# Attention heads issued in pairs on TensorE: scores in one step, values in the next

## The chip, the cores and the metric

The kernel runs on one core of one Trainium2 chip. The metric is the device time of one execution in microseconds. The kernel before took 1118.67 us in the median of three runs (1115.35, 1126.55 and 1118.67); the profiled execution, from which every row below comes, took 1115.28 us, of which 1113.6 us are its span.

## The reference

A trunk of two layers on 256 tokens of width 1024, all in fp32. Each layer is: half a SwiGLU, a mixer, half a SwiGLU, and a gated embedding; at the end a norm. The change concerns the mixers. Each has 16 heads of width 64:

```
# even layer (layer 0)
oa = forgetting_attention(...)        # 8 heads: softmax(q k / 8 + F_q - F_k, causal) v
ob = stick_breaking_attention(...)    # 8 heads: exp(log_sigmoid(z) + reversed running sum) v, no softmax
# odd layer (layer 1)
oc = chunked_relbias_attention(...)   # 8 heads: softmax(q k / 8 + bias[rel]) v
od = sliding_window_gqa(...)          # 8 query heads on 2 key/value heads, ALiBi, a sink in the softmax
x = x + concatenate([o_first, o_second]) @ w_out
```

For every head the kernel needs scores (q times k, contraction over the head's 64 dimensions, 128 + 256 columns for two row blocks of 128 tokens), something that makes weights of them, and values (weights times v: contraction over 128 tokens, 64 output dimensions, 256 + 128 columns).

## The kernel before

**Precision and storage.** The large products are split: weights and activations are each kept as a high and a low fp32r part, and a product is three matmuls (lines 1063 to 1065, helper `product`, and 1168 to 1170 in `token_tile`). The attention's own matmuls are plain fp32. In the trace each fp32 matmul stands as two MATMUL records, each behind a LDWEIGHTS record of its own; a transpose stands as one. q and k lie transposed (`qT`, `kT`: 128 partitions are the dimensions of two heads), so head 2p has partitions 0 to 63 and head 2p + 1 partitions 64 to 127 of the same tile. The output of values is transposed as well: head 2p writes partitions 0 to 63 and head 2p + 1 partitions 64 to 127 of one PSUM bank, and the even or odd pair picks the bank (`BANK_O`).

**Order of the work.** Each engine has its own program, written out by hand, and semaphores tie them. On TensorE the input projection (`mixer_in`) makes tiles of 128 output columns, each 24 matmuls; between the tiles lie attention steps. `attention_step(layer, i)` runs for i = 0 to 18. In layer 0 steps 0 to 11 each follow a tile of the input projection (the last 12 of 24 tiles), in layer 1 steps 0 to 10 (the last 11 of 19). The rest lie in `mixer_out`: there each step holds a half tile of the output projection (12 matmuls, `out_half`), passed in as `tile`, which is issued after the step's scores and ahead of the rest. Step i issues, in this order: the scores of head i, the tile if there is one, the middle part of head i - 1, the values of head i - 2.

**The middle part** is, for softmax heads, three transposes of the normalised weights (line 1263) into one bank, which ScalarE copies to `probsT` (line 670); for stick-breaking heads (layer 0, heads 8 to 15) it is three fp32 matmuls onto the scores' bank (1269 to 1271), whose exponential ScalarE writes to `probsT` (line 676). Scores of stick-breaking heads begin with two bf16 matmuls that write the mask (1248, 1249).

**The other engines.** VectorE (attention_step from line 930) evicts the tile, adds the bias and takes the row minimum of head i (line 951), splits weight chunks (746), normalises head i (965 to 970), and at even steps writes the low part of the output of a finished pair (979, semaphore `os_lo`). ScalarE takes the exponentials of head i (651, or 661 and 663), then copies head i - 1 to `probsT`, then at even steps writes the high part of the pair (680), then splits weights (511). Two waits matter below. The copy to `probsT` for head j waits until the values of head j - 2, which read the same buffer, are done (`pv_done`). The scores of head j wait until the bank of head j - 2 is free: for stick-breaking that is the exponential of line 676 (`sb_a`), for softmax the bias step of line 951 (`logits_ready`).

`out_half` for the first half uses the outputs of the pairs 0 to 3; for its first tile each product waits for `os_lo` of its pair.

Of the kernel before, what the change touches and what calls it, by code (L numbers as in the profile page):

```python
# [13 lines left out]
P = 128  # L14
D_MODEL, SEQ, D_FF, D_PLE, DEPTH = 1024, 256, 2816, 256, 2
HD = 64
# [13 lines left out]
LOGITS = 3 * P  # L30
# [92 lines left out]
def trunk(nc, x, p, ln_ffn1, w_ffn1_gu, w_ffn1_down, ln_mix, w_in_even, b_forget, w_out_even, w_in_odd,  # L123
# [14 lines left out]
    with ExitStack() as ctx:  # L138
# [15 lines left out]
        with ExitStack() as region:  # L154
            osp = region.enter_context(nc.sbuf_tensor("osp", [P, KD, 2, SEQ], F32R))
            qT = region.enter_context(nc.sbuf_tensor("qT", [P, 8, SEQ], F32))
            kT = region.enter_context(nc.sbuf_tensor("kT", [P, 8, SEQ], F32))
            vN = region.enter_context(nc.sbuf_tensor("vN", [P, TOK, 2 * GROUP_W], F32))
# [21 lines left out]
        probsT = sb("probsT", [P, 2, LOGITS], F32)  # L180
# [5 lines left out]
        mask_sb = sb("mask_sb", [P, P], BF16)  # L186
        identb = sb("identb", [P, P], BF16)
# [31 lines left out]
        ps = ctx.enter_context(nc.psum_tensor("ps", [P, 8, 512], F32))  # L219
        BANK_S, BANK_PT, BANK_F = 4, 6, 7  # L220
        BANK_O = (3, 7)
# [25 lines left out]
        scores_done, logits_ready = sem("scores_done"), sem("logits_ready")  # L247
        exp_done, pt_done, pt_ready = sem("exp_done"), sem("pt_done"), sem("pt_ready")
        sb_abs, sb_e, sb_log, sb_sp, incl_done, sb_a = sem("sb_abs"), sem("sb_e"), sem("sb_log"), sem("sb_sp"), sem("incl_done"), sem("sb_a")
        norm_step, probs_ready, pv_done = sem("norm_step"), sem("probs_ready"), sem("pv_done")  # L250
# [23 lines left out]
        heads = [(layer, group, h) for layer in range(DEPTH) for group in range(2) for h in range(HEADS)]  # L274
        is_sb = [layer == 0 and group == 1 for layer, group, h in heads]
        soft_no = [sum(not s for s in is_sb[:g]) for g in range(len(heads))]
        stick_no = [sum(is_sb[:g]) for g in range(len(heads))]

        def head_q(g):
            _, group, h = heads[g]  # L280
            r = HD * (h % 2)
            return slice(r, r + HD), 4 * group + h // 2

        def head_k(g):
            layer, group, h = heads[g]
            if layer == 1 and group == 1:
                return 4 if h // 4 == h % 2 else 5
            return 4 * group + h // 2

        def head_v(g):  # L290
            layer, group, h = heads[g]
            return GROUP_W * group + HD * (h // 4 if layer == 1 and group == 1 else h)
# [41 lines left out]
        def last_written(layer, want):  # L334

            return written(layer, max(n for n, t in enumerate(IN_TILES[layer]) if want(t[2], t[3])))
# [712 lines left out]
        def _(pe):  # L1049
# [178 lines left out]
            def scores(g):  # L1228
                layer, group, h = heads[g]
                s, (rows, qt), kt = g % 2, head_q(g), head_k(g)  # L1230
                S = ps[:, BANK_S + s]

                held = 4 if layer == 1 and group == 1 else kt
                pe.wait_ge(*last_written(layer, lambda what, idx: (what, idx) in (("q", qt), ("k", held))))
                if layer == 1 and group == 1 and kt == 5:
                    pe.wait_ge(k_swapped, 32)
                if g >= 2:

                    if is_sb[g - 2]:
                        pe.wait_ge(sb_a, stick_no[g - 2] + 1)  # L1240
                    else:
                        pe.wait_ge(logits_ready, 2 * (soft_no[g - 2] + 1))
                if not is_sb[g]:
                    for t, sl, keys in ((0, slice(0, P), P), (1, slice(P, LOGITS), SEQ)):
                        mm = pe.matmul(S[:, sl], qT[rows, qt, t * P:(t + 1) * P], kT[rows, kt, 0:keys], start=True, stop=True)  # L1245
                else:

                    pe.matmul(S[:, 0:P], identb[:], mask_sb[:], start=True, stop=True)
                    pe.matmul(S[:, 2 * P:LOGITS], identb[:], mask_sb[:], start=False, stop=True, skip_group_check=True)
                    pe.matmul(S[:, 0:SEQ], kT[rows, kt, 0:P], qT[rows, qt, :], start=False, stop=True, skip_group_check=True)  # L1250
                    mm = pe.matmul(S[:, 2 * P:LOGITS], kT[rows, kt, P:SEQ], qT[rows, qt, P:SEQ], start=False, stop=True,
                                   skip_group_check=True)
                mm.then_inc(scores_done, 1)

            def middle(g):
                s = g % 2
# [14 lines left out]
                    pe.matmul(S[:, SEQ:LOGITS], negtri[:], sp_[:, SEQ:LOGITS], start=False, stop=True,  # L1271
                              skip_group_check=True).then_inc(incl_done, 1)

            def values(g):
                s, v = g % 2, head_v(g)
                layer, group, h = heads[g]
                if layer == 1 and group == 1:
                    pe.wait_ge(*last_written(layer, lambda what, idx: what == "vd"))
                else:
                    pe.wait_ge(*last_written(layer, lambda what, idx: what == "v" and idx[:2] == (group, h // 4)))  # L1280
                if is_sb[g]:
                    pe.wait_ge(sb_a, stick_no[g] + 1)
                else:
                    pe.wait_ge(pt_ready, soft_no[g] + 1)


                pair, rows = g // 2, slice(HD * (g % 2), HD * (g % 2 + 1))
                if pair % KD < 2:
                    reuse(BANK_O[pair % 2])
                else:  # L1290
                    pe.wait_ge(os_lo, pair - 1)
                V = vN[:, :, v:v + HD]
                O = ps[rows, BANK_O[pair % 2], :]
                pe.matmul(O[:, 0:SEQ], V[:, 0], probsT[:, s, 0:SEQ], start=True, stop=False)  # L1294
                pe.matmul(O[:, P:SEQ], V[:, 1], probsT[:, s, SEQ:LOGITS], start=False, stop=True).then_inc(pv_done, 1)  # L1295

            def attention_step(layer, i, norm, tile=None):

                first, n = 2 * HEADS * layer, 2 * HEADS
                g = first + i  # L1300
                if i == 0:

                    pe.wait_ge(rstd_ready, norm + 1)
                    if layer == 0:
                        pe.wait_ge(bias_ready, HEADS)
                        pe.wait_ge(f_step, 4)
                    else:
                        pe.wait_ge(p_lo, 1)
                if i < n:
                    scores(g)  # L1310
                if tile is not None:
                    tile()
                if 1 <= i <= n:
                    middle(g - 1)
                if 2 <= i <= n + 1:
                    values(g - 2)
                if i == n + 2:
                    for b in range(2):
                        reader[BANK_O[b]] = (os_lo, (first + n) // 2 - 1 + b)
# [55 lines left out]
            for m in range(KD):  # L1375
                if m >= 4:
                    pe.wait_ge(resid, m - 3)
                for t in range(TOK):
                    mm = pe.transpose(ps[:, m % 4, t * P:(t + 1) * P], xin[:, t, m * P:(m + 1) * P], ident[:])
# [55 lines left out]
```

## Time and profile before

| | |
|---|---|
| runs, us | 1115.35, 1118.67, 1126.55; median 1118.67 |
| profiled execution, us | 1115.28, span 1113.6, mean granted TensorE clock 0.989 |
| TensorE matmul (PE) | busy 1080.0 us, 97% of the span |
| TensorE weight load (PEld) | busy 953.0 us, 86% |
| VectorE (DVE) | busy 773.6 us, 69% |
| ScalarE (ACT) | busy 590.3 us, 53% |
| GpSimd (POOL) | busy 82.8 us, 7% |

Times are microseconds unless marked ns, counted from the start of the span. A line number is a line of the kernel. The ends of matmuls are modelled, so two that follow each other overlap in the rows; what a matmul takes of the engine is the distance from its start to the start of the next. A row of the timeline may hold several records of one form: its start is that of the first, its length reaches to the end of the last.

### The profile page before, as it was taken

The numbers are of one execution on the slowest core, as the hardware profiler recorded it, in microseconds if no ns is written. First come the engines' busy times: TensorE is split into PE (matmuls) and PEld (weight loads), VectorE is DVE, ScalarE is ACT, GpSimd is POOL, SyncE is SP. The second block draws the span as 40 slices with busy tenths as digits, with TensorE's granted clock in tenths as the row PEclk, the third lists the DMA queues.
The fourth block names the chain that finished last, engine by engine and source line by source line (L and its number), as shares of the span: only waits on it lengthen the run. The fifth ranks groups of instructions, "written<-read, shape, count | busy, mean of one in ns | idle before, by whom it ended". The sixth has DMA issues, their size and how long they took to land.

```text
span 1113.6 us, 18550 instructions
## 1 busy us (share of the span) xinstructions
PE 1080.0 (97%) x6691; PEld 953.0 (86%) x6691; DVE 773.6 (69%) x1361; ACT 590.3 (53%) x1027; POOL 82.8 (7%) x112
## 2 busy tenths in 40 slices
PE   4999999999999999999999999998999999999996
PEld 3888888998888888888888888888987888888886
DVE  5887855666545887855689777667657698785566
ACT  5565545434445565545556565444555566554454
POOL 4000001000002000001020000014003200000102
PEclk9999999999999999999999999999999999999998
DMA  8656447563232756447546554566623275544731
GB/s 258 217 191 204 130 139 222 186 194 114 87 104 60 234 188 208 130 137 224 189 152 227 190 187 143 154 203 207 202 81 114 85 227 187 190 129 136 212 128 39
DMA packets 225848, 183.94 MB, mean 165 GB/s; under 512 B 4648, under 2 KB 224512, under 8 KB 225792
## 3 DMA queue, kind: packets, MB, share of 16 engines
q1 hardware_dynamic: 222688, 181.45, 52.0%
q10 hardware_dynamic: 3104, 1.77, 0.6%
q8 instruction: 32, 0.52, 0.2%
q14 instruction: 24, 0.20, 0.1%
HBM read 182.02 MB, written 1.06 MB: 164 GB/s over the span
## 4 chain that ended last, share of the span: by engine, by line
PE 89%; DVE 5%; issue 3%; ACT 2%; DMA 0%; SPq 0%; DVEq 0%; POOLq 0%; POOL 0%; ACTq 0%
PE ps L1072 43%; PE ps L1073 22%; PE ps L1063 5%; PE ps L1064 4%; PE ps L1065 4%; DVE wsp L746 2%; PE ps L1245 2%; PE ps L1294 2%; PE ps L1168 1%; PE ps L1169 1%; PE ps L1170 1%; ACT wsp L511 1%; PE ps L1263 1%; PE ps L1295 1%; DMA gin<-in_ln_final_dram 0%
## 5 line engine op out<-in xcount | busy, mean ns | idle before, releaser
L746 DVE TENSOR_TENSOR wsp<-raw,wsp 128x1024 fp32r<-128x1024 f32 (+1 forms) x382 | 423.3, 1124 | 69.1 <-ACT wsp L511 62.7
L1072 PE MATMUL ps<-xsA,wsp 128*128 128x512 f32 x1056 | 372.7, 397 | 4.5 <-DVE wsp L746 3.9
L511 ACT ACTIVATE wsp<-raw 128x1024 fp32r<-128x1024 f32 (+1 forms) x382 | 356.0, 958 | 32.4 <-PE ps L1065 30.1
L1073 PE MATMUL ps<-xsA,wsp 128*128 128x256 f32 x1056 | 296.8, 281 | 0.0
L1072 PE MATMUL ps<-hff,wsp 128*128 128x512 f32 x704 | 245.4, 394 | 0.0
L1072 PEld LDWEIGHTS ps<-xsA,wsp 128*128 128x128 f32 x1056 | 198.9, 188 | 52.2 <-issue 5.2
L1073 PEld LDWEIGHTS ps<-xsA,wsp 128*128 128x128 f32 x1056 | 200.7, 190 | 0.0
L1073 PE MATMUL ps<-hff,wsp 128*128 128x256 f32 x704 | 196.7, 279 | 0.0
L1072 PEld LDWEIGHTS ps<-hff,wsp 128*128 128x128 f32 x704 | 131.9, 187 | 30.4
L1073 PEld LDWEIGHTS ps<-hff,wsp 128*128 128x128 f32 x704 | 132.8, 189 | 0.0
L1072 PE MATMUL ps<-xsB,wsp 128*128 128x512 f32 x352 | 124.2, 398 | 2.3 <-DVE xsB L810 2.1
L761 DVE TENSOR_TENSOR sq<-ps,sq 128x512 f32<-128x512 f32 x88 | 60.5, 687 | 86.0 <-ACT sq L527 86.0
L1063 PE MATMUL ps<-xsA,wsp 128*128 128x256 f32 x360 | 106.8, 297 | 3.4 <-DVE wsp L746 3.4
L571 ACT ACTIVATE xsA<-xT,gains 128x256 fp32r<-128x256 f32 x56 | 28.4, 507 | 152.1 <-DVE xT L872 126.8
L527 ACT ACTIVATE sq<-ps 128x512 f32<-128x512 f32 x88 | 51.9, 589 | 106.4 <-PE ps L1073 106.4
L1064 PE MATMUL ps<-xsA,wsp 128*128 128x256 f32 x360 | 104.0, 289 | 0.0
L1065 PE MATMUL ps<-xsA,wsp 128*128 128x256 f32 x360 | 103.8, 288 | 0.0
L1073 PE MATMUL ps<-xsB,wsp 128*128 128x256 f32 x352 | 98.1, 279 | 0.0
L1072 PEld LDWEIGHTS ps<-xsB,wsp 128*128 128x128 f32 x352 | 66.7, 190 | 18.5 <-DVE xsB L810 2.6
L530 ACT ACTIVATE silu<-gate_n 128x256 f32<-128x256 f32 x88 | 36.8, 419 | 84.9 <-DVE gate_n L763 84.9
L1063 PEld LDWEIGHTS ps<-xsA,wsp 128*128 128x128 f32 x360 | 71.2, 198 | 5.8 <-DVE wsp L746 3.6
L1064 PEld LDWEIGHTS ps<-xsA,wsp 128*128 128x128 f32 x360 | 71.3, 198 | 0.1
(172 smaller groups left out, 1328.4 us busy)
## 6 DMA issues: line engine op xcount, KB each, us to landing
raw<-in_w_ffn_gu_dram SPq DMA_DIRECT2D x88, 1024.0 KB, 5.1
raw<-in_w_ffn_down_dram SPq DMA_DIRECT2D x64, 704.0 KB, 4.7
raw<-in_w_in_even_dram SPq DMA_DIRECT2D x12, 1024.0 KB, 5.4
raw<-in_w_in_odd_dram SPq DMA_DIRECT2D x9, 1024.0 KB, 5.3
raw<-in_w_ple_gate_dram SPq DMA_DIRECT2D x8, 1024.0 KB, 5.9
raw<-in_w_out_even_dram SPq DMA_DIRECT2D x4, 1024.0 KB, 5.2
raw<-in_w_out_odd_dram SPq DMA_DIRECT2D x4, 1024.0 KB, 5.2
raw<-in_w_ple_proj_dram SPq DMA_DIRECT2D x2, 1024.0 KB, 5.1
```

What stands on the lines that cost most here:

```text
L511: act.activation(wsp[:, s, 0, half * n:(half + 1) * n], raw[:, s, half * n:(half + 1) * n], ACT.Copy).then_inc(hi, 1)
L527: act.activation(cross[:], ps[:, b:b + 3:2, SEQ:], ACT.Copy).then_inc(gu_cross, 1)
L530: act.activation(silu[:], gate_n[:, 0], ACT.Silu).then_inc(gu_silu, 1)
L571: act.activation(stream(norm)[:, m, 0, :], xT[:, m], ACT.Copy, scale=gain(norm, m)).then_inc(xs_hi, 1)
L746: dve.tensor_tensor(wsp[:, s, 1, sl], raw[:, s, sl], wsp[:, s, 0, sl].bitcast(F32), ALU.subtract).then_inc(lo, 1)
L761: dve.tensor_tensor(cross[:], ps[:, b:b + 3:2, 0:SEQ], cross[:], ALU.add).then_inc(gu_sum, 1)
L1063: pe.matmul(out_, whi, moving[:, 0, :], start=first, stop=False)
L1064: pe.matmul(out_, whi, moving[:, 1, :], start=False, stop=False)
L1065: return pe.matmul(out_, wlo, moving[:, 0, :], start=False, stop=last)
L1072: pe.matmul(ps[:, bank, :], whi, moving.rearrange("p s t -> p (s t)"), start=first, stop=False)
L1073: return pe.matmul(ps[:, bank, SEQ:], wlo, moving[:, 0, :], start=False, stop=last)
L1245: mm = pe.matmul(S[:, sl], qT[rows, qt, t * P:(t + 1) * P], kT[rows, kt, 0:keys], start=True, stop=True)
```

## The change

Softmax heads' scores are issued for two heads at once, at even steps (`scores_pair`): first the 128-column part of head g, then that of head g + 1, then the 256-column parts in the same order. The scores of stick-breaking heads stay one head a step (`scores`). Values of all heads are issued for two heads at once, at odd steps from step 3 on (`values_pair`, for heads i - 3 and i - 2): the 256-column parts of both, then the 128-column parts of both. The waits follow: a pair of scores waits for `logits_ready` of head g - 1, and a pair of values for the `probsT` of both heads. The middle part, the programs of the other engines and the number of matmuls are as before.

```diff
--- before.py
+++ after.py
@@ -1230,27 +1230,37 @@
                 s, (rows, qt), kt = g % 2, head_q(g), head_k(g)
                 S = ps[:, BANK_S + s]
 
-                held = 4 if layer == 1 and group == 1 else kt
-                pe.wait_ge(*last_written(layer, lambda what, idx: (what, idx) in (("q", qt), ("k", held))))
-                if layer == 1 and group == 1 and kt == 5:
+                pe.wait_ge(*last_written(layer, lambda what, idx: (what, idx) in (("q", qt), ("k", kt))))
+                if is_sb[g - 2]:
+                    pe.wait_ge(sb_a, stick_no[g - 2] + 1)
+                else:
+                    pe.wait_ge(logits_ready, 2 * (soft_no[g - 2] + 1))
+
+                pe.matmul(S[:, 0:P], identb[:], mask_sb[:], start=True, stop=True)
+                pe.matmul(S[:, 2 * P:LOGITS], identb[:], mask_sb[:], start=False, stop=True, skip_group_check=True)
+                pe.matmul(S[:, 0:SEQ], kT[rows, kt, 0:P], qT[rows, qt, :], start=False, stop=True, skip_group_check=True)
+                pe.matmul(S[:, 2 * P:LOGITS], kT[rows, kt, P:SEQ], qT[rows, qt, P:SEQ], start=False, stop=True,
+                          skip_group_check=True).then_inc(scores_done, 1)
+
+            def scores_pair(g):
+
+                layer, group, h = heads[g]
+                kinds = [("q", head_q(g)[1])] + [("k", 4 if layer == 1 and group == 1 else head_k(g))]
+                pe.wait_ge(*last_written(layer, lambda what, idx: (what, idx) in kinds))
+                if layer == 1 and group == 1:
                     pe.wait_ge(k_swapped, 32)
                 if g >= 2:
-
-                    if is_sb[g - 2]:
-                        pe.wait_ge(sb_a, stick_no[g - 2] + 1)
+                    if is_sb[g - 1]:
+                        pe.wait_ge(sb_a, stick_no[g - 1] + 1)
                     else:
-                        pe.wait_ge(logits_ready, 2 * (soft_no[g - 2] + 1))
-                if not is_sb[g]:
-                    for t, sl, keys in ((0, slice(0, P), P), (1, slice(P, LOGITS), SEQ)):
-                        mm = pe.matmul(S[:, sl], qT[rows, qt, t * P:(t + 1) * P], kT[rows, kt, 0:keys], start=True, stop=True)
-                else:
-
-                    pe.matmul(S[:, 0:P], identb[:], mask_sb[:], start=True, stop=True)
-                    pe.matmul(S[:, 2 * P:LOGITS], identb[:], mask_sb[:], start=False, stop=True, skip_group_check=True)
-                    pe.matmul(S[:, 0:SEQ], kT[rows, kt, 0:P], qT[rows, qt, :], start=False, stop=True, skip_group_check=True)
-                    mm = pe.matmul(S[:, 2 * P:LOGITS], kT[rows, kt, P:SEQ], qT[rows, qt, P:SEQ], start=False, stop=True,
-                                   skip_group_check=True)
-                mm.then_inc(scores_done, 1)
+                        pe.wait_ge(logits_ready, 2 * (soft_no[g - 1] + 1))
+                for t, sl, keys in ((0, slice(0, P), P), (1, slice(P, LOGITS), SEQ)):
+                    for e in (g, g + 1):
+                        rows, qt = head_q(e)
+                        mm = pe.matmul(ps[:, BANK_S + e % 2, sl], qT[rows, qt, t * P:(t + 1) * P], kT[rows, head_k(e), 0:keys],
+                                       start=True, stop=True)
+                        if t == 1:
+                            mm.then_inc(scores_done, 1)
 
             def middle(g):
                 s = g % 2
@@ -1271,28 +1281,30 @@
                     pe.matmul(S[:, SEQ:LOGITS], negtri[:], sp_[:, SEQ:LOGITS], start=False, stop=True,
                               skip_group_check=True).then_inc(incl_done, 1)
 
-            def values(g):
-                s, v = g % 2, head_v(g)
+            def values_pair(g):
+
                 layer, group, h = heads[g]
                 if layer == 1 and group == 1:
                     pe.wait_ge(*last_written(layer, lambda what, idx: what == "vd"))
                 else:
                     pe.wait_ge(*last_written(layer, lambda what, idx: what == "v" and idx[:2] == (group, h // 4)))
                 if is_sb[g]:
-                    pe.wait_ge(sb_a, stick_no[g] + 1)
+                    pe.wait_ge(sb_a, stick_no[g] + 2)
                 else:
-                    pe.wait_ge(pt_ready, soft_no[g] + 1)
-
-
-                pair, rows = g // 2, slice(HD * (g % 2), HD * (g % 2 + 1))
+                    pe.wait_ge(pt_ready, soft_no[g] + 2)
+                pair = g // 2
                 if pair % KD < 2:
                     reuse(BANK_O[pair % 2])
                 else:
                     pe.wait_ge(os_lo, pair - 1)
-                V = vN[:, :, v:v + HD]
-                O = ps[rows, BANK_O[pair % 2], :]
-                pe.matmul(O[:, 0:SEQ], V[:, 0], probsT[:, s, 0:SEQ], start=True, stop=False)
-                pe.matmul(O[:, P:SEQ], V[:, 1], probsT[:, s, SEQ:LOGITS], start=False, stop=True).then_inc(pv_done, 1)
+                for e in (g, g + 1):
+                    rows = slice(HD * (e % 2), HD * (e % 2 + 1))
+                    pe.matmul(ps[rows, BANK_O[pair % 2], 0:SEQ], vN[:, 0, head_v(e):head_v(e) + HD], probsT[:, e % 2, 0:SEQ],
+                              start=True, stop=False)
+                for e in (g, g + 1):
+                    rows = slice(HD * (e % 2), HD * (e % 2 + 1))
+                    pe.matmul(ps[rows, BANK_O[pair % 2], P:SEQ], vN[:, 1, head_v(e):head_v(e) + HD], probsT[:, e % 2, SEQ:LOGITS],
+                              start=False, stop=True).then_inc(pv_done, 1)
 
             def attention_step(layer, i, norm, tile=None):
 
@@ -1306,14 +1318,16 @@
                         pe.wait_ge(f_step, 4)
                     else:
                         pe.wait_ge(p_lo, 1)
-                if i < n:
+                if i < n and is_sb[g]:
                     scores(g)
+                elif i < n and i % 2 == 0:
+                    scores_pair(g)
                 if tile is not None:
                     tile()
                 if 1 <= i <= n:
                     middle(g - 1)
-                if 2 <= i <= n + 1:
-                    values(g - 2)
+                if i >= 3 and i % 2 == 1:
+                    values_pair(g - 3)
                 if i == n + 2:
                     for b in range(2):
                         reader[BANK_O[b]] = (os_lo, (first + n) // 2 - 1 + b)
```

## Rows read from the trace of the kernel before

**Rows 1.** The page: busy time of engines, then chain of waits.

```profile
PE 1080.0 (97%) x6691; PEld 953.0 (86%) x6691; DVE 773.6 (69%) x1361; ACT 590.3 (53%) x1027; POOL 82.8 (7%) x112
...
PE 89%; DVE 5%; issue 3%; ACT 2%; DMA 0%; SPq 0%; DVEq 0%; POOLq 0%; POOL 0%; ACTq 0%
```

**Rows 2.** PE's waits by releaser, 300:345 (total, times, longest).

```profile
PE ps L1248 <- ACT probsT L676: 0.4, 1, 0.4
```

**Rows 3.** Windows, PE alone, layer 0's steps 0, 1, 3 (length, busy).

```profile
256.52:260.41 3.89, 3.89 (x28) 1.00 0.03 10
260.41:264.61 4.20, 4.20 (x32) 1.00 0.06 10
...
269.81:275.00 5.19, 5.19 (x37) 1.00 0.22 60
```

**Rows 4.** Timeline, PE, scores of layer 0's step 0 (start, length, operation).

```profile
256.10 0.28 PE L1064 MATMUL ps<-xsA,wsp 128*128 128x256 f32 x1
256.22 0.28 PE L1065 MATMUL ps<-xsA,wsp 128*128 128x256 f32 x1
256.52 0.89 PE L1245 MATMUL ps<-kT,qT 64*128 64x128 f32 x4
257.34 0.39 PE L1063 MATMUL ps<-xsA,wsp 128*128 128x256 f32 x1
257.57 0.28 PE L1064 MATMUL ps<-xsA,wsp 128*128 128x256 f32 x1
```

**Rows 5.** Timeline of PE, layer 1's step 10, one head's scores, transposes, values.

```profile
842.04 0.92 PE L1245 MATMUL ps<-kT,qT 64*128 64x128 f32 x4
842.89 0.55 PE L1263 MATMUL ps<-ident,probs 128*128 128x128 f32 x3
843.37 0.65 PE L1294 MATMUL ps<-probsT,vN 128*64 128x256 f32 x2
843.85 0.38 PE L1295 MATMUL ps<-probsT,vN 128*64 128x128 f32 x2
844.16 0.92 PE L1245 MATMUL ps<-kT,qT 64*128 64x128 f32 x4
```

**Rows 6.** Weight loads (PEld) of the same scores and values.

```profile
842.04 0.52 PEld L1245 LDWEIGHTS ps<-kT,qT 64*128 64x128 f32 x4
...
843.64 0.35 PEld L1295 LDWEIGHTS ps<-probsT,vN 128*64 128x64 f32 x2
```

**Rows 7.** Lines by form, scores and values (count; busy, mean ns).

```profile
L1245 PE MATMUL ps<-kT,qT 64*128 64x256 f32 x48 | 14.3, 377 | 0.0
...
L1295 PE MATMUL ps<-probsT,vN 128*64 128x128 f32 x64 | 12.2, 273 | 0.0
```

**Rows 8.** Timeline of PE, layer 0, end of step 12 and start of 13.

```profile
319.77 0.65 PE L1294 MATMUL ps<-probsT,vN 128*64 128x256 f32 x2
...
320.56 0.23 PE L1248 MATMUL ps<-mask_sb,identb 128*128 128x128 bf16 x1
```

**Rows 9.** Timeline of ACT, exponentials after the middle of steps 12, 13.

```profile
319.88 0.49 ACT L676 ACTIVATE probsT<-ps 128x384 f32<-128x384 f32 x1 [0.82 <-PE ps L1271]
...
324.33 0.47 ACT L676 ACTIVATE probsT<-ps 128x384 f32<-128x384 f32 x1
```

**Rows 10.** Timeline of PE, layer 1, the waiting product of step 11.

```profile
846.52 0.39 PE L1063 MATMUL ps<-osp,wsp 128*128 128x256 f32 x1 [0.18 <-DVE osp L979]
```

**Rows 11.** Timeline of DVE, layer 1, steps 9 to 12.

```profile
836.95 0.42 DVE L903 SCALAR_TENSOR_TENSOR qT<-ps,rstd 128x256 f32<-128x256 f32 x1 [0.87 <-PE ps L1065]
...
840.32 0.63 DVE L970 TENSOR_SCALAR probs<-probs,rinv 128x128 f32<-128x128 f32 x2
...
846.06 0.41 DVE L979 TENSOR_TENSOR osp<-ps,osp 128x256 fp32r<-128x256 f32 x1
...
850.90 0.34 DVE L951 CUSTOM_DVE_ANT_0 probs<-ps,bias_swa,nsink 128x128 f32<-128x128 f32 x1
...
853.09 0.55 DVE L970 TENSOR_SCALAR probs<-probs,rinv 128x128 f32<-128x128 f32 x2
```

## The prediction

> **What bounds the kernel now.** I read the page first: TensorE is busy 97% of the span, and the chain of waits lies on it for 89% [rows 1]. The next question is whether it is also the bound inside the mixers, where the change lies. TensorE's waits there are few: one of 0.4 us in layer 0 (the scores of head 12 wait for line 676) [rows 2], and one of 0.18 us idle, with a restart behind it, in layer 1 (step 11's product waits for line 979) [rows 10]. The windows of single steps show TensorE busy for all of 3.89, 4.20 and 5.19 us [rows 3]. So a microsecond taken from TensorE's queue in the mixers shortens the span until another engine's result is late.
>
> Where the time of a step goes is read from starts. In the projection a record of 256 columns follows the last after 0.12 us. Into the scores it is 0.30 us, the scores take 0.82 us to the next group, and the record after that comes 0.23 us later instead of 0.12 [rows 4]. Inside the scores the loads of four records span 0.52 us, the last one being 0.19 long, so they follow each other at 0.11 us [rows 6]. That is also what a 128-column fp32 record takes. The last 256-column record starts 0.92 - 0.38 = 0.54 us in and the next group at 0.85, so 0.31 lies between them [rows 5, 7]; 0.54 is an exposed first load (0.10), two steps of 0.11 and one of 0.22. **Bare streaming of one head's scores** is thus 2 x 0.11 + 2 x 0.215 = 0.65 us. The rest appears wherever the shape used of the array changes (128 x 128, 64 x 128 for scores, 128 x 64 for values): about 0.09 us after the last record, and a weight load that nothing hides, 0.10 us for 128 columns and 0.05 for 64 (the two 256-column records of values take 0.48 us, not 0.43 [rows 5]). Step 0 is one tile (24 x 0.12 = 2.87) and one visit to the scores, 3.89 - 2.87 = 1.02, so the two shape changes of that visit cost 0.36. Step 1 adds transposes, 0.31, about bare streaming: they share the tile's shape. Step 3 adds values, 5.19 - 4.20 = 0.99, of which 0.34 are shape changes [rows 3].
>
> **The change, part by part.**
>
> Fewer shape changes. Twelve visits for scores (24 softmax heads in pairs) and sixteen for values (32 heads) go away: 12 x 0.36 + 16 x 0.34 = 9.8 us. In layer 1's part of the output projection values are followed directly by scores and share a change; there are 5 such seams before and 2 after, so 3 x 0.17 = 0.5 is not gained. **9.3 us.** No wait and no instruction is added for it; the streaming of the second head stays, 0.65 us.
>
> Work on two halves. No row shows matmuls on different halves of the array next to each other, so this is bounded from both sides. Upper end of gain: starts stay in order, weight loads stay 0.11 (128 columns) or 0.05 us apart, each half does one record at a time, but the second record of one matmul and the first of the next run side by side. For scores the starts are then 0, 0.21, 0.32, 0.43, 0.54, 0.76, 0.77, 0.98 and the next group at 1.29 instead of 1.50: 0.21 a pair, little because the loads are the bound. For values 0, 0.27, 0.28, 0.49, 0.50, 0.61, 0.71, 0.82, next group at 1.02 instead of 1.44: 0.43 a pair. In all 12 x 0.21 + 16 x 0.43 = 9.4 us. Lower end: each of the three changes of half in a pair costs what a change of shape does, 0.19 (scores) and 0.14 (values): 12 x 3 x 0.19 + 16 x 3 x 0.14 = 13.6 us of loss. In between: nothing, if records only queue. I take the **gain of 9.4 us**, because the nearest rows show loading ahead at work whenever the shape stays: loads 0.19 us long follow each other at 0.11 under the matmuls [rows 6], and loads and matmuls are busy for 86% and 97% of one span [rows 1].
>
> The same rows set a rule against half of this. The Trainium skill, in "TensorE: Matmul & The Clock Gate", Part 3, says that a weight load overlaps a running matmul only when the row group differs; the halves for values share the row group. By that the values' 6.9 us would be nothing and the sum 8 us. The trace disagrees with it where the whole array is used: there too loads and matmuls run at once [rows 1].
>
> New waits in layer 0's output part (steps 11 to 16). The scores of head g wait for the exponential of head g - 2, which ScalarE starts after the middle part of the step before. Before, 0.79 us of values lay between that middle part and the scores [rows 8], and the exponential (0.49 us, beginning 0.11 us after the values did [rows 8, 9]) was ready at 320.37 with the mask at 320.56: just covered. After, even steps hold no values, so at the start of steps 13 and 15 TensorE stands still for about 0.75 us. At the end of odd steps the exponential also waits until head g - 4's values are read, which now are the first of the pair in the same step: finished 1.3 us after the pair begins without overlap (0.9 with it), exponential and signals 0.6, pair over at 1.44 (1.02): 0.5 us at the starts of steps 12 and 14, where 0.4 stood at the first. Together 2.5 less the old 0.4: **2.1 us lost.** Inside the input projection a tile of 2.87 us lies between, and nothing waits.
>
> Layer 1, step 11. The fourth product waits for `os_lo` of the fourth pair, which VectorE writes at 846.06 + 0.41 after the whole chain of step 10 [rows 11]; TensorE came at 846.2 and went on at 846.52 [rows 10]. That chain starts from head 10's scores, now 0.22 us later (two records of head 11 lie ahead of its second part). TensorE now does only the pair of scores (1.50), transposes (0.39) and nine products (1.08) from 842.04 on and arrives at 845.0; it goes on at 846.75. **1.3 us lost** against the free-running sum, 1.5 with overlap. After it VectorE paces: head 12's normalised weights come at 853.09 + 0.55 = 853.64 from a bias step at 850.90 that follows VectorE's own queue, not TensorE [rows 11]. TensorE reaches them at 853.9 without overlap, at 853.3 with it: 0.3 lost with overlap.
>
> What costs nothing, and its cover. In layer 1's projection steps the chain of head 8 and later is longest: eviction at 836.95 to 840.95, 4.0 us [rows 11], 4.2 with the later scores; TensorE needs scores, transposes and the next tile first, 1.3 to 1.5 + 0.33 + 2.87 = 4.5 to 4.7. Cover 0.3 us; gone, every such step would wait. ScalarE's copy to `probsT` at odd steps now waits for the first head of the pair in the same step, about 1.8 us after the tile, but its own exponentials end about there, 2.0 us after; the weight splits queued behind it do not move. DMAs are untouched.
>
> Sum, likeliest case: 9.3 + 9.4 - 2.1 - 1.8 = **14.8 us** less than 1115.28, that is 1100.5. The profiled execution equals the lowest run and lies 3.4 us below the median; I put half of it on top: **1102**.
>
> **The rivals** (times with the same 2 us on top).
>
> *No overlap.* Records on different halves queue at 0.11 and 0.215 us. 9.3 - 2.1 - 1.3 = 5.9: 1111. For: every pair of neighbours in the trace queues. Against: none of them is on different halves. Chance 0.24.
>
> *Scores overlap, values don't* (the rule above): 9.3 + 2.5 - 2.1 - 1.6 = 8.1: 1109. Chance 0.10.
>
> *Changing halves drains* (the other sign). Place: the three changes in each of 28 pairs, 84 in all. Price 0.14 to 0.19 us each: -5.9 + 13.6 = +7.7: 1125. It decides from 5.9 / 84 = 0.07 us per change. For: a change of shape does cost that. Against: here only the place changes. Chance 0.12. The Trainium skill, "TensorEngine Tiling (Array Packing)", Key Properties, says that changing the mode drains and changing the tile does not; its first half agrees with [rows 4, 5], no row here shows the second.
>
> *Waits eat the overlap.* The 0.3 us of cover in layer 1's projection steps is too small and VectorE paces, there and in layer 0's output part: 5 us more in waits, 1107. For: both are near in [rows 11]. Against: softmax heads without a sink have a shorter chain. Chance 0.08.
>
> **How the numbers follow.** The forecast has 0.46. A measurement of this kernel can tell about 1% (11 us) from no change. The overlap case lies 15 us off, so most of it is faster: 0.42, and 0.03 from the others; slower by over 1% needs the drain at its upper price or something I have not seen: 0.08; the rest, 0.47, is within 1%. The range takes in overlap, none, and the waits, with the median's scatter of a few us, and leaves out the drain: 1098 to 1122.
>
> **What would show it.** After: in a pair, the first 256-column record of head g + 1 starts about 0.01 us after the second of head g (overlap) or 0.215 (none) or more than 0.3 (drain). Two steps of layer 0 take 10.39 us now and should take 9.06 (9.70, 10.6). TensorE's waits should show the mask matmul of stick-breaking scores waiting for line 676 four times, 2.5 us, and step 11's product about 1.5 to 1.7 us. Wrong would be the prediction if stages outside the mixers change by more than 2 us, or if line 951 or 970 releases TensorE.

## The result, and the profile after

The changed kernel took 1101.44 us in the median of four runs (1099.68 to 1107.96), the kernel before 1119.14 us of four (1115.35 to 1126.55): a ratio of 0.985, interval 0.981 to 0.988. Timed again later beside the kernel before on another chip the ratio was 0.983 (0.979 to 0.987). The profiled execution took 1100.13 us, span 1097.3.

The waits of TensorE in the whole span, of the changed kernel (total, times, longest), those that lie in the mixers:

```profile
PE ps L1239 <- ACT probsT L676: 2.8, 4, 0.7
...
PE ps L1273 <- DVE probs L970: 2.3, 3, 1.2
...
PE ps L1063 <- DVE osp L979: 2.0, 1, 2.0
```

Before there stood 0.4 us in the first of these three lines [rows 2], nothing in the second, and 0.18 us in the third [rows 10]. The waits outside the mixers are the same in both kernels within 0.1 us, but for the first of all, for a DMA, 9.8 us here and 9.1 before. Now one pair, the timeline of PE in layer 0's step 2 and the following step 3, and PEld for the same stretches:

```profile
266.04 0.28 PE L1065 MATMUL ps<-xsA,wsp 128*128 128x256 f32 x1
266.25 0.93 PE L1260 MATMUL ps<-kT,qT 64*128 64x128 f32 x8
...
270.36 0.49 PE L1273 MATMUL ps<-ident,probs 128*128 128x128 f32 x3
270.78 0.65 PE L1302 MATMUL ps<-probsT,vN 128*64 128x256 f32 x4
271.26 0.39 PE L1306 MATMUL ps<-probsT,vN 128*64 128x128 f32 x4
271.58 0.39 PE L1063 MATMUL ps<-xsA,wsp 128*128 128x256 f32 x1
```

```profile
266.25 0.52 PEld L1260 LDWEIGHTS ps<-kT,qT 64*128 64x128 f32 x8
...
270.78 0.20 PEld L1302 LDWEIGHTS ps<-probsT,vN 128*64 128x64 f32 x4 [0.17 <-issue]
271.05 0.36 PEld L1306 LDWEIGHTS ps<-probsT,vN 128*64 128x64 f32 x4
```

Eight records of scores take 0.93 us where four took 0.92, and from the first values to the second (256 columns, then 128) it is 0.48 us for two heads as for one [rows 5]. The loads show the same: eight in 0.52 us, as four did [rows 6]. The second head of a pair costs TensorE almost nothing. From the first start to the next group a pair of scores takes 0.856 us (one head: 0.850) and a pair of values 0.800 (one head: 0.794). Two steps of layer 0, as windows of PE (stretch, length, busy time and records, granted clock, DMA share, GB/s):

```profile
266.25:270.40 4.15, 4.15 (x37) 1.00 0.83 255
270.40:274.65 4.25, 4.25 (x38) 1.00 0.17 47
```

Together 8.40 us, against 2 x 5.19 [rows 3].

**The mixers, measured alone.** From the first scores of a layer to the first matmul behind its last values, the kernel before ends at these rows of PE, layer 0 (from 256.52, [rows 4]) and layer 1:

```profile
339.35 0.39 PE L1063 MATMUL ps<-osp,wsp 128*128 128x256 f32 x1
...
792.89 0.37 PE L1245 MATMUL ps<-kT,qT 64*128 64x128 f32 x1
...
867.75 0.39 PE L1063 MATMUL ps<-osp,wsp 128*128 128x256 f32 x1
```

and the changed kernel at

```profile
259.12 0.38 PE L1260 MATMUL ps<-kT,qT 64*128 64x128 f32 x2
...
333.07 0.39 PE L1063 MATMUL ps<-osp,wsp 128*128 128x256 f32 x1
...
786.88 0.38 PE L1260 MATMUL ps<-kT,qT 64*128 64x128 f32 x2
...
851.45 0.39 PE L1063 MATMUL ps<-osp,wsp 128*128 128x256 f32 x1
```

Layer 0's mixer went from 82.83 to 73.95 us and layer 1's from 74.86 to 64.57: 19.2 us less. The span fell by 16.3, because stages that the change does not touch took 2.9 us longer in this execution: 259.12 stands where 256.52 stood. Such differences occur between executions of one and the same kernel: the changed kernel took 958.8 us outside its mixers in this execution and 950.8 in that of e11 below. Over all the profiled runs the stretch ahead of layer 0's first scores took 253.2 to 259.8 us, the one between the mixers 451.9 to 462.2, and the one behind layer 1's values 242.5 to 246.3, while mixers that an experiment leaves as they are repeat within 0.3. So the experiments are read by these two stretches, which I call the mixers; they come from the same rows of each profile.

### The profile page after: what moved, and what is told of

Its sections match the earlier page's. It is cut to its first block and busy times, and to the rows that moved or that the text cites. A ratio compares the mean times of both kernels' runs of the same rounds, so it can differ in the third digit from the quotient of the medians.

```text
span 1097.3 us, 18523 instructions
## 1 busy us (share of the span) xinstructions
PE 1056.0 (96%) x6691; PEld 939.4 (86%) x6691; DVE 773.1 (70%) x1361; ACT 590.3 (54%) x1027; POOL 82.7 (8%) x112
```

## The experiments

Mixers in us (layer 0, layer 1, sum), and for timed runs the ratio to the kernel before with its interval:

| kernel | layer 0 | layer 1 | sum | ratio |
|---|---|---|---|---|
| before | 82.8 | 74.9 | 157.7 | |
| changed | 73.9 | 64.6 | 138.5 | 0.985 (0.981 to 0.988) |
| e1 grouped | 74.0 | 64.8 | 138.8 | 0.986 (0.981 to 0.992) |
| e2 same half | 80.4 | 71.5 | 151.8 | 0.996 (0.994 to 0.998) |
| e3 scores only | 78.9 | 69.3 | 148.2 | |
| e4 values only | 77.9 | 69.4 | 147.3 | |
| e5 four buffers | 72.9 | 64.5 | 137.4 | |
| e6 outputs first | 73.9 | 64.4 | 138.3 | |
| e7 tile first | 70.9 | 64.6 | 135.5 | |
| e8 combined | 70.9 | 63.7 | 134.7 | 0.980 (0.977 to 0.983) |
| e9 no sink | 73.9 | 61.6 | 135.5 | |
| e10 vector order | 70.9 | 62.2 | 133.1 | 0.978 (0.975 to 0.981) |
| e11 change again | 73.9 | 64.8 | 138.7 | 0.983 (0.979 to 0.987) |

**e1: does the order inside a pair matter?**

```diff
-                for t, sl, keys in ((0, slice(0, P), P), (1, slice(P, LOGITS), SEQ)):
-                    for e in (g, g + 1):
-                        rows, qt = head_q(e)
+                for e in (g, g + 1):
+                    rows, qt = head_q(e)
+                    for t, sl, keys in ((0, slice(0, P), P), (1, slice(P, LOGITS), SEQ)):
...
(values_pair: one loop over the two heads, both matmuls of a head inside it)
```

> As the changed kernel, but within a pair both matmuls of the first head are issued before those of the second. Theory A (each half of the array is fed on its own, the order of issue within a pair does not matter): as the changed kernel, a pair of scores 0.86 us and a pair of values 0.80 us from its first start to the next group, span 1097 +- 3 us. Theory B (starts keep the order of issue, so only a record and its direct neighbour on the other half can meet): only the last record of the first head meets the first of the second, a pair of scores about 1.4 us, of values about 1.3 us, some 15 us more streaming, of which about 5 us go into waits that exist anyway: span about 1107 us.

Theory A. The timeline of PE of this kernel:

```profile
271.87 0.93 PE L1260 MATMUL ps<-kT,qT 64*128 64x128 f32 x8
272.73 0.55 PE L1273 MATMUL ps<-ident,probs 128*128 128x128 f32 x3
...
276.40 0.66 PE L1302 MATMUL ps<-probsT,vN 128*64 128x256 f32 x4
276.89 0.39 PE L1304 MATMUL ps<-probsT,vN 128*64 128x128 f32 x4
```

0.93 us for eight records again, although the second head's are all issued behind the first head's. A pair of scores takes 0.864 us to the next group. The first two records alone, a window cut short behind their starts, in e1 and in e2 below:

```profile
271.87 0.39 PE L1260 MATMUL ps<-kT,qT 64*128 64x128 f32 x2
...
272.40 0.37 PE L1260 MATMUL ps<-kT,qT 64*128 64x128 f32 x1
```

In e1 the records start in twos, 13 to 14 ns apart and 0.1 to 0.2 us from two to two; in the alternating order the twos are 6 to 7 ns apart. A record does not name its half. I read each two as one record of each head, since the two are alike in columns and length, and on one half (e2) there is a single start where there are two here. So the alternation within a pair is not what the change gains by; that the heads lie on different halves, next to each other in TensorE's program, is, as e2 shows.

**e2: the fewer shape changes alone.**

```diff
-                        rows, qt = head_q(e)
+                        rows, qt = slice(0, HD), head_q(e)[1]
...
-                    rows = slice(HD * (e % 2), HD * (e % 2 + 1))
+                    rows = slice(0, HD)
(values of the second head behind both matmuls of the first)
```

> As the changed kernel, but both heads of a pair use the first half of the array: scores read partitions 0 to 63 for both, values of both go to partitions 0 to 63 one head after the other, so the second head of each pair is not computed. It has the change's fewer changes of shape and its order of steps, without work side by side. Theory (gain = fewer shape changes 9.3 us + overlap 18 us - waits): pair of scores 1.50 us, pair of values 1.44 us, waits about 3.5 us, span 6 us below the kernel before, 1107 to 1110 us. Rival (the gain is the overlap alone; changes of shape cost nothing that is saved): span 1113 us or more.

```profile
272.40 1.57 PE L1260 MATMUL ps<-kT,qT 64*128 64x128 f32 x8
...
277.58 0.65 PE L1302 MATMUL ps<-probsT,vN 128*64 128x256 f32 x2
278.06 0.38 PE L1304 MATMUL ps<-probsT,vN 128*64 128x128 f32 x2
278.28 0.59 PE L1302 MATMUL ps<-probsT,vN 128*64 128x256 f32 x2
```

On one half the records queue: 1.50 us to the next group for scores, 1.44 for values. The mixers are 5.9 us shorter than before, the net of the shape changes and the waits that stand here (0.7 us twice for line 676, 1.6 for line 979). The other 13.3 us of the change's 19.2 are work side by side, net of the further waits that it brings. The span, 1106.8 us, is just under the expected 1107 to 1110.

**e3 and e4: each half of the change.**

```diff
 # e3: scores paired, values at every step
-                if i >= 3 and i % 2 == 1:
-                    values_pair(g - 3)
+                if 2 <= i <= n + 1:
+                    (values of head g - 2 alone)
 # e4: values paired, scores at every step
-                elif i < n and i % 2 == 0:
-                    scores_pair(g)
+                elif i < n:
+                    (scores of head g alone, waiting for head g - 2)
```

> Only the scores are paired; values of head i - 2 are issued at every step as before. Theory: 12 visits x (0.36 + 0.64) = 12 us less, no new wait in layer 0, in layer 1 about 1 us more at step 11's product and in the product of the steps behind it: span 1102 to 1104 us. If the new waits came from the paired scores, the scores of stick-breaking heads would wait 2.5 us or more here too.

> Only the values are paired, the scores are issued one head a step. Theory: 16 visits x (0.34 + 0.64) = 15.7 us less, four waits of the stick-breaking scores for their exponentials (2.8 us in all, as in the changed kernel), about 1 us more wait at layer 1's step 11: span 1100 to 1103 us. If those waits came from the paired scores they would be gone here.

The mixers lose 9.5 us in e3 and 10.4 in e4 (19.9 together, 19.2 in the change). In layer 0, four pairs of scores give 3.98 us, the 4.0 of the theory with no new wait. In layer 1 both have about 1 us for line 979, as expected, and smaller waits that were not: 1.3 us of new waits in e3 and 3.8 in e4 in all. The sums of 12.0 and 15.7 then leave 10.7 and 11.9, and 1.2 and 1.5 us are still missing. About 0.5 of each is a slip in what I expected: in layer 1's output part three visits fewer save one change of shape each and not two, as the prediction had it. The rest I put down to restarts, what TensorE loses behind a wait beyond the idle time; that is argued and not shown. e3's span, 1108.7 us, missed the expected 1102 to 1104: its mixers gained 2.5 us less than the sum, and outside them it took 4.6 us more than the kernel before. e4's span, 1099.7 us, is just under the expected 1100 to 1103, with 3.5 us less outside the mixers than the kernel before. Waits of PE in e4:

```profile
PE ps L1239 <- ACT probsT L676: 2.8, 4, 0.7
...
PE ps L1063 <- DVE osp L979: 1.0, 1, 1.0
```

The 2.8 us for line 676 are all here; in e3 they are 0.4. They come from the paired values.

**e5 and e7: the waits in layer 0.** In the changed kernel, ScalarE and PE at the end of step 11:

```profile
308.87 0.52 ACT L663 ACTIVATE probs<-probs 128x384 f32<-128x384 f32 x1
309.60 0.49 ACT L676 ACTIVATE probsT<-ps 128x384 f32<-128x384 f32 x1 [0.20 <-PE ps L1306]
```

```profile
308.64 0.65 PE L1302 MATMUL ps<-probsT,vN 128*64 128x256 f32 x4
309.12 0.39 PE L1306 MATMUL ps<-probsT,vN 128*64 128x128 f32 x4
310.23 0.22 PE L1239 MATMUL ps<-mask_sb,identb 128*128 128x128 bf16 x1 [0.72 <-ACT probsT L676]
```

ScalarE is held 0.20 us by the pair of values, then the mask matmul by ScalarE. At the end of an even step nothing but the middle part lies between (the wait is 0.67 us).

```diff
 # e5
-        probsT = sb("probsT", [P, 2, LOGITS], F32)
+        probsT = sb("probsT", [P, 4, LOGITS], F32)
...
-                    if g - 1 >= 2:
-                        act.wait_ge(pv_done, g - 2)
+                    if g - 1 >= 4:
+                        act.wait_ge(pv_done, g - 4)
 # e7
+                lead = tile is not None and i < n and is_sb[g]
+                if lead:
+                    tile()
                 if i < n and is_sb[g]:
                     scores(g)
```

> As the changed kernel, with four probsT buffers in place of two, so ScalarE's copy for head j waits for the values of head j - 4 (over by then) and not for those of the pair that TensorE has just begun. Theory (at the ends of odd steps the exponential is late because it waits for pv_done of the pair in the same step; at the ends of even steps because nothing covers it): of the four waits of the mask matmul for line 676 two, those after a pair of values, fall from 0.7 us to nearly 0, two stay at 0.7; layer 0's mixer 1.4 us shorter, 72.5 us from its first scores to the end of its last values instead of 73.94. Rival (ScalarE's own queue, the exponentials of the next head, is what is late): all four waits stay.

> As the changed kernel, but in layer 0's output part (steps 12 to 15) the half tile of the output projection is issued ahead of the stick-breaking scores, so 1.5 us of work lies between the middle part and the scores that wait for its exponential. Theory: all four waits for line 676 go (2.8 us), nothing else is late, since TensorE comes back to the middle part 3.5 us after the scores and the chain of VectorE and ScalarE between takes 2.3 us: layer 0's mixer 70.9 to 71.4 us instead of 73.94. Rival (the waits move to the middle part, for line 975): under 1 us gained.

e5 left 1.8 us in three waits and gained 1.0 us in layer 0, not 1.4: one of the two falls only to about 0.4, since there ScalarE's own line 663 is late, as it was before the change [rows 2]. So both theory and rival hold a part of one wait. e7 removed all four, 2.8 us, and gave 3.0 us, the upper end of what was expected; the 0.2 us more I put down to restarts behind the waits, which is argued.

**e6, e9, e10: what holds layer 1.**

```diff
 # e6: ScalarE's output copy moved ahead of its exponentials, VectorE's behind the bias step
+                if 3 <= i and (g - 3) % 2 == 1:
+                    (osp high or low part)
...
 # e9: e6 without
-                            for t in range(TOK):
-                                act.activation(sinkexp[...], nsink[...], ACT.Exp, ...)
-                        step(dve.tensor_tensor(rowsum[:, slot], rowsum[:, slot], sinkexp[:, slot], ALU.add))
```

> As the changed kernel, but ScalarE and VectorE write the high and low part of a finished pair's output at the head of the even step (ScalarE before its exponentials, VectorE right behind the bias step) and not at its end: the pair is complete since the odd step. Theory (step 11's product waits for the tail of VectorE's chain of step 10, not for the values): the wait of 2.0 us for line 979 goes to 0; VectorE's normalising in the same step comes 0 to 0.4 us later, so of the 2 us about 1 us comes back as more wait for line 970 in layer 1's output part, where VectorE paces: layer 1's mixer 63.0 to 64.2 us instead of 64.57. Rival (the values of the fourth pair themselves are late): the wait stays.

> As e6 (output parts first), but the sink is left out of the sliding-window heads: ScalarE's two sinkexp instructions (0.46 us) and VectorE's addition to the row sum (0.16 to 0.45 us) are gone for each of the 8 heads, TensorE's work is the same. It shortens the chain from a head's bias step to its normalised weights by about 0.65 us. Theory (layer 1's output part is paced by that chain, run head after head on VectorE): the waits for line 975 fall from 3.1 us to under 1.2, layer 1's mixer from 64.36 to 62.0 to 62.8 us. Rival (something else, the exponentials' copy or the order on TensorE, paces it): unchanged within 0.3 us.

Waits of PE in e6:

```profile
PE ps L1273 <- DVE probs L975: 3.1, 2, 1.6
```

The wait for the output part is gone, but the layer is only 0.2 us shorter. Most of the 2 us came back in waits for the normalised weights (line 970 of the changed kernel is 975 here), and a part of it is TensorE's clock. In four of the profiled executions the granted clock fell to the lower of its two levels, 1.2 GHz, for 3.4 us inside layer 1's mixer: in e1, e5 and e11 after the wait of 2.0 us for line 979, in e6 after two waits of 1.5 and 1.6 us for line 975. In the changed kernel's first profiled execution and in e7, with the same wait of 2.0 us, it stayed at 2.4 GHz. Windows of PE over one pair of scores and twelve products, in e11 and in the changed kernel's first execution, then in e6 and in e9 (length, busy time and records, mean granted clock, DMA):

```profile
828.43:832.15 3.72, 3.72 (x22) 0.60 0.27 91
...
833.42:835.82 2.40, 2.40 (x22) 1.00 0.49 169
...
842.31:846.22 3.91, 3.91 (x22) 0.56 0.10 33
...
841.37:843.75 2.38, 2.38 (x22) 1.00 0.41 137
```

In e11 TensorE lost 1.3 us in this stretch, but layer 1's mixer took only 0.2 us longer than in the first execution of the same kernel: the waits for line 970 fell from 2.3 to 1.0 us. That is a first sign that VectorE paces this part. In e6 the clock fell later, and the loss was not covered. The last normalised weights of e6 and the transposes that read them:

```profile
849.48 0.55 DVE L975 TENSOR_SCALAR probs<-probs,rinv 128x128 f32<-128x128 f32 x2
...
850.74 0.49 PE L1273 MATMUL ps<-ident,probs 128*128 128x128 f32 x3
```

The weights were ready at 850.03, and TensorE came 0.7 us later. By my estimate it would have waited for them at the full clock, so about 0.7 us of the 64.4 are the clock's, and e6's order is worth 0.9 us, with 1.1 of the 2 coming back, about as expected. What paces is seen on VectorE, here of the changed kernel, step 13 (start, length, idle before):

```profile
839.51 0.34 DVE L951 CUSTOM_DVE_ANT_0 probs<-ps,bias_swa,nsink 128x128 f32<-128x128 f32 x1
...
841.35 0.16 DVE L965 TENSOR_TENSOR rowsum<-rowsum,sinkexp 128x2 f32<-128x2 f32 x1 [1.08 <-ACT sinkexp L656]
841.54 0.17 DVE L968 RECIPROCAL rinv<-rowsum 128x2 f32<-128x2 f32 x1
841.75 0.55 DVE L970 TENSOR_SCALAR probs<-probs,rinv 128x128 f32<-128x128 f32 x2
842.21 0.42 DVE L987 TENSOR_TENSOR xT<-ps,xT 128x256 f32<-128x256 f32 x1
842.54 0.35 DVE L951 CUSTOM_DVE_ANT_0 probs<-ps,bias_swa,nsink 128x128 f32<-128x128 f32 x1
```

A head takes 3.03 us on VectorE (839.51 to 842.54), and for 1.08 of them it waits for ScalarE's exponentials with the next head's bias step and the residual's addition queued behind. The two scores that TensorE now delivers together are worked off one after the other. e9 shortened that chain without touching TensorE, and layer 1's mixer fell from 64.4 to 61.6 us. Without the 0.7 us of e6's clock that is 2.1 us less, inside the expected 1.6 to 2.4. The waits for the normalised weights stayed at 2.0 us, where under 1.2 were expected. The chain is the bound there. e10 does it without leaving work out.

```diff
 # e8 = e6 + e7 + layer 1's steps from 11 on: values_pair ahead of middle
 # e10 = e8 and, on VectorE
                 advance(units)
+                if add is not None:
+                    add()                # the half tile's addition to xT, line 987
                 (then the wait for the exponentials and the normalising)
...
+                    if m:
                         advance(2 * (ph.c0 + RING))
```

> The changed kernel with the output parts written first (e6), the tile first in layer 0 (e7), and in layer 1's output part the pair of values ahead of the transposes of its step, which gives VectorE's normalising 0.65 us more. Theory: waits for lines 676 and 979 gone, for 970 about 1 us: layer 0's mixer 71.2 us, layer 1's 62.5 to 63.5 us, together 4 to 5 us below the changed kernel, about 1.9% below the kernel before. Rival (VectorE's queue in layer 1 gives all of it back): layer 1 stays at 64.5 us.

> As e8 (output parts first, tile first in layer 0, values ahead of transposes in layer 1's output part), and VectorE adds the half tile to the residual (0.42 us) and makes the split of step 12 (1.21 us) while it waits for ScalarE's exponentials, not after the normalising. Theory (VectorE's queue, head after head, paces layer 1's output part): its period falls by 0.3 to 0.4 us a head and once by 1.2: layer 1's mixer 61.5 to 62.7 us instead of 63.74, layer 0's unchanged at 70.9. Rival (ScalarE, or TensorE by now, paces): 63.4 us or more.

> The changed kernel itself, unaltered, timed on the same chip as e10 so that the two can be compared. All theories: 1.5% below the kernel before, mixers 73.9 and 64.6 us.

e11 repeated the change with 73.9 and 64.8 us, where 73.9 and 64.6 were expected. e8 gained 3.9 us in the mixers over the change: layer 0 as expected, layer 1 at 63.7 a little short of it, and no shorter than my estimate for e6 without its clock. By that estimate values ahead of the transposes bought nothing: TensorE now waits for ScalarE's copy to `probsT`, which stands behind the next head's exponentials in ScalarE's program (the profile calls this wait "issue"):

```profile
837.02 0.47 ACT L674 ACTIVATE probsT<-ps 128x384 f32<-128x384 f32 x1
...
837.59 0.65 PE L1302 MATMUL ps<-probsT,vN 128*64 128x256 f32 x4 [1.53 <-issue]
```

In e10 layer 1 fell to 62.2, the middle of what was expected, and a head takes 2.70 us on VectorE where it took 3.03:

```profile
837.30 0.35 DVE L951 CUSTOM_DVE_ANT_0 probs<-ps,bias_swa,nsink 128x128 f32<-128x128 f32 x1
...
840.00 0.35 DVE L951 CUSTOM_DVE_ANT_0 probs<-ps,bias_swa,nsink 128x128 f32<-128x128 f32 x1
```

The ratio of e10 to the kernel before is 0.978 (0.975 to 0.981), that of the unaltered change on the same chip 0.983 (0.979 to 0.987), with medians of 1092.17 and 1096.35 us. The intervals overlap a little, so for the whole program the step from the change to e10 is likely and not shown; in the mixers, 133.1 against 138.7 us, it is shown.

## Why the prediction was right

The forecast was 1102 us; 1101.44 was measured, 15.2 us less between the profiled executions against a sum of 14.8. The kind of thing that happens was right: fewer changes of shape, work side by side, new waits in both output parts. Of the four terms only the waits in layer 0 came out in size. The others were off, and cancelled.

*Fewer shape changes, 9.3 us less the waits.* Right in kind, somewhat too high. The rival without overlap said 5.9 and e2, which is that case, measured 5.9 in the mixers, but the agreement is partly chance. Its waits were fewer than that rival had them (line 676 twice and not four times: a pair of values of 1.44 us covers the exponential), 2.3 us above those of before where the rival had 3.4. With them put back the shape changes give 8.2 us. Restarts do not close the gap to 9.3, since the kernel before has two waits with restarts of its own against three in e2. What does stays open.

*Work on two halves, 9.4 us.* That the halves work side by side was right; what I had as the limit was wrong, and with it the size by half. I had starts in the order of issue and loads for both halves in one line, 0.11 us apart. The trace shows neither: 12 pairs of scores save 0.64 to 0.65 us each (about 1.50 to 0.856) and 16 of values 0.64 (1.444 to 0.800), **18.0 us**. The bound I called the upper end of the gain was not one; the loads that I argued from [rows 6] were all on one place, and say nothing of two. The first 256-column record of head g + 1 starts 0.21 us ahead of the second of head g, which is none of the three signs I had written down, and the two steps take 8.40 us and not 9.06. The Trainium skill's rule in "TensorE: Matmul & The Clock Gate", Part 3, that a weight load overlaps a running matmul only when the row group differs, does not hold for these values: same row group, and the loads for the 128-column parts take 0.36 us for both heads where one head's take 0.35 [rows 6]. What the Trainium skill says in "TensorEngine Tiling (Array Packing)", Key Properties, that different tiles can load weights and multiply in parallel, agrees with the pairs, 0.856 us for two heads against 0.850 for one.

*New waits in layer 0, 2.5 us.* Right in place, number and size: four, 2.8 us. The cover that values gave to the exponential went away as [rows 8, 9] had it.

*Layer 1, 1.8 us.* The place was right, the size not: 4.1 us of idle time more than before. Step 11's product waited 2.0 us, where I had 1.5 to 1.7, because TensorE came there 0.65 us earlier than in my sum without overlap and 0.43 earlier than with the overlap I had. The waits for line 970, which I had at 0.3 us, are 2.3 in this execution (1.0 in e11, where the fallen clock takes the place of the rest). So VectorE eats a part of the overlap, as the last rival had it, but in layer 1's output part. Where that rival placed it, it did not come: in the projection steps the cover of 0.3 us held, and in layer 0's output part TensorE waits for ScalarE.

Put together, 8.2 + 18.0 would be gained without waits, 6.5 us went into new waits (2.4 in layer 0, 4.1 in layer 1) where I had 3.9, and the 0.5 us that then lack to the measured 19.2 are perhaps restarts.

That the sum came out near the measurement is thus largely luck: 8.6 us too little overlap, against 1.1 too much for the shape changes, 2.6 too few waits, the 0.5 just named, and 2.9 us of drift outside the mixers, which is no effect of the change; together they leave the 16.3 us by which the span fell. Two slips in the working change little: a pair of values gains 0.42 us by its own starts and not 0.43, and two steps with drains add up to 10.7 and not 10.6. By my own last sentence the prediction would even be wrong, since both signs I named there appeared. Line 970 releases TensorE, and that is a real miss. The stages outside the mixers changed by 2.9 us, but that sign was badly chosen: two executions of the changed kernel differ by 8.0 us there. The rivals: drains at a change of half are excluded (6 ns between the starts of the two halves). The case in which only scores overlap is excluded by e4, where pairs of values take 0.80 us.

## What to carry to other kernels

In this kernel two small fp32 matmuls that use different halves of the array, by rows or by columns, cost the time of one if they stand next to each other in TensorE's program, and the order within the pair makes no difference (e1). Each visit to another shape of the array costs 0.3 to 0.35 us here for going and coming back, so group visits even when nothing can run side by side (e2: 5.9 us less). When TensorE gets a large part of a stage for free, look at once for the engine that works off its results one by one: in layer 1 the next clear gain, about 1.5 us from e8 to e10, came from VectorE's order alone. And before you read a few tenths of a microsecond out of one profiled execution, look at the granted clock in the same stretch: in e6 it hid most of what the experiment had gained.

## What the runs showed of the hardware that was not expected

The two halves do not share one line of starts. By the reading of the twos given with e1, the second head's first record starts 13 to 14 ns after the first head's first, and 0.2 us ahead of the first head's second record, although it is issued behind all four of them. Weight loads of the two halves run at once as well: eight in 0.52 us, where four on one half take 0.52. TensorE's granted clock fell for 3.4 us after a wait of 2.0 us in three executions (e1, e5, e11) and stayed up after the same wait in two (the changed kernel's first, e7).
